# The third mixer's input products in three rounded passes, its weights through the ring of pieces, and the recurrence's rates moved ahead of the queries

## The reference

```python
def even_mixer_2(h, pos, w_in, conv_w, conv_b, w_a, b_a, w_i, b_i, lam, q_norm, k_norm, sinks, w_out):
    proj = h @ w_in                       # h is the normed input, w_in is 1024 x 1792
    xb, gate, q, k, v = jnp.split(proj, cuts, axis=-1)      # 512, 512, 512, 128, 128 columns
    y_lru = rg_lru(xb, conv_w, conv_b, w_a, b_a, w_i, b_i, lam) * jax.nn.gelu(gate)
    q = rope(rms_norm_2(q.reshape(bsz, seq, 8, 64), q_norm), pos)
    k = rope(rms_norm_2(k.reshape(bsz, seq, 2, 64), k_norm), pos)
    y_att = sliding_window_attention(q, k, v, sinks)
    return jnp.concatenate([y_lru, y_att], axis=-1) @ w_out

def rg_lru(xb, ...):
    xc = causal_depthwise_conv_2(xb, conv_w) + conv_b
    r = sigmoid(xc by 8 blocks @ w_a + b_a);  gi = sigmoid(xc by 8 blocks @ w_i + b_i)
    log_a = -8.0 * r * softplus(-lam)
    a = exp(log_a);  u = sqrt(-expm1(2 log_a)) * (gi * xc)
    h_t = a_t * h_(t-1) + u_t             # a scan over the tokens
```

## Time and profile before

| | us |
|---|---|
| median of 3 runs | 2619.16 (2617.56 to 2625.74) |
| the profiled execution | 2622.34 |
| its span | 2620.5 |
| PE busy in the span | 2438.7 (93%) |
| DVE, ACT, POOL busy | 1805.9, 1424.2, 321.3 |
| stage mix2, first input product to the start of its attention | 1079.2 to 1134.3 |

### The profile page before, as it was taken

The page is one execution under the profiler, slowest core; times in us unless marked ns, Lnnn a source line. Parts: engine busy times, 40 slices in busy tenths (PEclk is TensorE's granted clock), DMA queues, the critical chain, the costliest instruction groups (busy, mean ns, idle before and its releaser), DMA issues. The chain is left out here.

```text
span 2620.5 us, 40002 instructions
## 1 busy us (share of the span) xinstructions
PE 2438.7 (93%) x15188; PEld 2039.8 (78%) x15188; DVE 1805.9 (69%) x2444; ACT 1424.2 (54%) x1900; POOL 321.3 (12%) x215
## 2 busy tenths in 40 slices
PE   7889889989897999989998996899999999999998
PEld 6447569989885799757997985788888888888886
DVE  3665554557575555574556764889989988889986
ACT  4242243445552444343435542677778787877776
POOL 4110200014442000000003431000000000000000
PEclk9889999999899999979998997899999999999999
DMA  7510325544231454414544402899999999999995
GB/s 256 174 47 21 128 97 191 176 142 152 97 129 65 138 177 166 165 65 145 192 160 168 155 2 93 322 373 383 378 384 367 389 376 381 377 379 377 377 381 214
DMA packets 180011, 573.86 MB, mean 219 GB/s; under 512 B 11966, under 2 KB 81726, under 8 KB 136764
## 3 DMA queue, kind: packets, MB, share of 16 engines
q1 hardware_dynamic: 175932, 558.27, 57.4%
q0 software_dynamic: 2992, 11.01, 1.6%
q10 hardware_dynamic: 976, 3.03, 0.3%
HBM read 564.16 MB, written 6.29 MB: 218 GB/s over the span
## 5 line engine op out<-in xcount | busy, mean ns | idle before, releaser
L3487 DVE TENSOR_TENSOR moe_weights_low<-ring,moe_weights_high 128x1024 fp32r<-128x1024 f32 x672 | 780.4, 1221 | 95.3 <-ACT moe_weights_high L3736 95.2
L3736 ACT CAST moe_weights_high<-ring 128x1024 fp32r<-128x1024 f32 x672 | 686.7, 1053 | 109.1 <-PE banks L258 106.1
L256 PE MATMUL banks<-moe_weights_high,moe_rows_high 128*128 128x512 f32 x896 | 355.7, 397 | 3.1 <-DVE moe_rows_low L3492 2.5
L258 PE MATMUL banks<-moe_weights_low,moe_rows_high 128*128 128x512 f32 x896 | 350.9, 392 | 0.0
L257 PE MATMUL banks<-moe_weights_high,moe_rows_low 128*128 128x512 f32 x896 | 350.2, 391 | 0.0
L256 PE MATMUL banks<-ffn_x_high,ffn_weights_high 128*128 128x256 f32 x1056 | 299.5, 284 | 0.7 <-DVE ffn_x_low L3110 0.7
L257 PE MATMUL banks<-ffn_x_high,ring_low 128*128 128x256 f32 x1056 | 298.0, 282 | 0.0
L258 PE MATMUL banks<-ffn_x_low,ffn_weights_high 128*128 128x256 f32 x1056 | 297.7, 282 | 0.0
L3286 DVE TENSOR_TENSOR ring_low<-ring,ffn_weights_high 128x2048 fp32r<-128x2048 f32 x60 | 134.8, 2289 | 127.7 <-ACT ffn_weights_high L3260 127.7
L256 PEld LDWEIGHTS banks<-ffn_x_high,ffn_weights_high 128*128 128x128 f32 x1056 | 199.6, 189 | 4.2 <-DVE ffn_x_low L3110 1.3
L257 PEld LDWEIGHTS banks<-ffn_x_high,ring_low 128*128 128x128 f32 x1056 | 199.9, 189 | 2.7
(11 more groups left out here) (626 smaller groups left out, 4632.1 us busy)
## 6 DMA issues: line engine op xcount, KB each, us to landing
ring<-in_moe_gate_pieces SPq DMA_DIRECT2D x112, 1024.0 KB, 7.1
ring<-in_moe_up_pieces SPq DMA_DIRECT2D x112, 1024.0 KB, 7.4
ring<-in_moe_down_pieces SPq DMA_DIRECT2D x112, 1024.0 KB, 7.2
ring<-in_ffn_w SPq DMA_DIRECT2D x66, 1024.0 KB, 7.7
ring<-in_od_w_in SPq DMA_DIRECT2D x10, 2048.0 KB, 8.2
ring<-in_o_w_in SPq DMA_DIRECT2D x8, 2048.0 KB, 8.5
ring<-in_e_ffn_w_gate SPq DMA_DIRECT2D x11, 1024.0 KB, 5.4
ring<-in_e_ffn_w_up SPq DMA_DIRECT2D x11, 1024.0 KB, 7.9
```

Source lines behind the costliest of these rows:

```text
L256: pe.matmul(out_, lh, rh, start=start, stop=False)
L258: return pe.matmul(out_, lh, rl, start=False, stop=stop)
L3487: dve.tensor_tensor(lo[:, b], piece, hi[:, b].bitcast(F32), ALU.subtract).then_inc(sems["lo_done"], 1)
L3736: act.copy(hi[:, b * 1024:(b + 1) * 1024], piece).then_inc(sems["hi_done"], 1)
```

## The change

The product `project_parts` is cut in two: `begin_parts` makes the pieces and can split the first of them early, and `project_parts` can take what has been begun. All four input products of the stage become three-pass products on `x_parts`. Two of the first product's pieces are split inside the norm. After the first piece of keys and values the four pieces of the queries are split (`during={0: ...}`); after the third piece of the queries the four pieces of the gate product (`during={2: gate_early}`). `decay_rates` and `one_less` are emitted ahead of the queries' product, and `square_root` becomes the first entry of the attention's `during` list. In `project_parts` both token tiles of a product end together, with the last piece.

```diff
-        def project_parts(lhs, n_k, w, n_cols, ready, take, first_col=0, after=None, during={}):
+        def begin_parts(n_k, w, n_cols, first_col, after=None):
             rows = P
             chunk = 512 if n_k <= 8 else 256
...
+            def first_pieces(count):
+                for i in range(count):
+                    split_one(i)
+                for i in range(count):
+                    parts_ready[i] = split[i][2]()
+            return pieces, split, parts_ready, slot_of_chunk, split_one, first_pieces
+
+        def project_parts(lhs, n_k, w, n_cols, ready, take, first_col=0, after=None, during={}, begun=None):
+            rows = P
+            begun = begin_parts(n_k, w, n_cols, first_col, after) if begun is None else begun
+            pieces, split, parts_ready, slot_of_chunk, split_one, first_pieces = begun
+
             def first_piece():
-                split_one(0)
-                parts_ready[0] = split[0][2]()
+                first_pieces(1)
...
-        def turned_parts(w, first_col, n_tiles):
+        def turned_parts(w, first_col, n_tiles, ahead=2):
...
             def early():
-                for i in range(2):
+                for i in range(ahead):
                     split_one(i)
-                for i in range(2):
+                for i in range(ahead):
                     parts_ready[i] = split[i][2]()
...
-            normed = norm_turned(h, D, None, xT, g_in, params_landed, lambda: None)
+            w_in = a["e_w_in_2"][0]
+            first_early, first_product = turned_parts(w_in, 0, NT4)
+            normed = norm_turned(h, D, None, x_parts, g_in, params_landed, first_early)
+            top[0] = keep
...
-            conv_project(a["e_w_in_2"][0], 0, NT4, taps, bias, params_landed, normed, ACT.Identity, finish)
+            conv_project(w_in, 0, NT4, taps, bias, params_landed, normed, ACT.Identity, finish, first_product)
...
-            project(xT, KD, a["e_w_in_2"][0], 2 * KVH * N, normed, copy_out(qkv[:, :, H * N:]), first_col=2 * LW + H * N)
+            query_parts = begin_parts(KD, w_in, H * N, 2 * LW)
+            project_parts(x_parts, KD, w_in, 2 * KVH * N, normed, copy_out(qkv[:, :, H * N:]), first_col=2 * LW + H * N,
+                          during={0: lambda: query_parts[-1](4)})
...
             def take_queries(ps, mark, t, c0, n):
                 if t == 0:
-                    decay_rates()
-
                     @block.scalar
...
-                sums = query_sums(0, made["queries"])
-                one_less()
-                query_scaled(0, sums)
+                query_scaled(0, query_sums(0, made["queries"]))
...
-            project(xT, KD, a["e_w_in_2"][0], H * N, normed, take_queries, first_col=2 * LW)
-            sums = query_sums(1, V.at())
-            square_root()
-            rotated = query_scaled(1, sums)
+            decay_rates()
+            one_less()
+            gate_early, gate_product = turned_parts(w_in, LW, NT4, 4)
+            project_parts(x_parts, KD, w_in, H * N, normed, take_queries, first_col=2 * LW, during={2: gate_early},
+                          begun=query_parts)
+            rotated = query_scaled(1, query_sums(1, V.at()))
...
-            project_turned(a["e_w_in_2"][0], LW, NT4, normed, take)
+            gate_product(w_in, LW, NT4, normed, take)
...
-                                    const("band"), sinks, [lambda: None, inputs, gated_scan])
+                                    const("band"), sinks, [square_root, inputs, gated_scan])
```

More of the change, by code:

```diff
@@ L4054, in take @@
                 return S.at()
-            project_turned(a["e_w_in_2"][0], LW, NT4, normed, take)
+            assert top[0] <= ARENA - KD * T - PIECES * PIECE, top[0]
+            gate_product(w_in, LW, NT4, normed, take)
             gate_ready = S.at()
             have = paired_attention(qkv, H, KVH, N, N ** -0.5, lambda i: y[:, :, i * N:(i + 1) * N], rotated,
-                                    const("band"), sinks, [lambda: None, inputs, gated_scan])
+                                    const("band"), sinks, [square_root, inputs, gated_scan])
             lru_ready = made["lru"]
```

## The result

The changed kernel takes 2631.44 us (median of 6 runs, 2628.0 to 2636.08) against 2621.33 for the kernel before in the same comparison: a ratio of 1.004, 95% interval 1.0025 to 1.0055. It is slower, by 10.1 us at the medians. The interval (6.6 to 14.4 us) is clear of zero; its lower end lies under the 0.3%, 7.9 us, that the prediction counts as no change, and its middle over it. One of the six runs before took 5200.5 us and stands outside the ratio; the other five have a median of 2619.16, and the 15 to 20 runs of the kernel before in each later comparison have medians of 2620.48 to 2623.44. The profiled execution has a span of 2630.0, 9.5 more than before.

A forecast was written before the change was run, and what follows sets the result against it. VectorE's queue was taken to set the stage's end; +6.4 us to decay_rates, +2.6 to the rotation and +0.65 in the attention made +9.7, so 2628.9 us from the median 2619.2, range 2619 to 2637.

The forecast's parts named there:

- L968 at 1143: Sign for being right: VectorE's last rotation in the stage at 1143 us; before 1138 would show the prediction wrong.
- What bounds: In mix2, VectorE's queue, fed by ScalarE and TensorE, sets the stage's end, though TensorE looks full.
- The norm: Start of the stage: a subtraction and eight L445 make x^T ready at 1081.5 us, +2.3.
- The first product: After the norm: product takes 11.4 us, VectorE's convolutions set x_ready, which does not move; nothing gained.
- The keys' wait: Keys and values: casts queue behind the convolution's last copy, TensorE idles 5.5 us, product ends +3.9 us.
- half clock: Keys' product after TensorE's idleness: five us at clock 0.50 add 2.5 us, bounds 0 and 5.7.
- Rates to rotation: From decay_rates to rotated: 29.3 us instead of 26.7, +2.6, including 4.3 for two gate subtractions.
- The attention: square_root's 5.3 us mostly fill VectorE's 4.74 us idle before its first scores; +0.65 us, bounds 0 and 2.
- The lock: VectorE and GpSimd on shared SBUF ports: slowing each other is shown, a full lock for the whole instruction is not.
- The whole pace arrives: Rival: TensorE's queue sets the stage's end, so its savings arrive; about -6 us, 2613; chance 7%.
- Covered: Rival: subtractions at 1.23 and 2.41 alone, no clock drop; +5 to +6 us, 2625, no measurable change; chance 35%.

The follow-up runs named there:

- e1: Changed kernel with the two pieces of keys and values split inside the first product; stage 103.7 us, ratio 1.0044 to the kernel before.
- e8: Kernel before with all but one reciprocal of square_root's VectorE work moved into the attention's first round; 2615.97 us, ratio 0.9977, stage 91.5 us.
- e2: Changed kernel with all 14 subtractions of the stage on VectorE, none on GpSimd; stage 103.4 us, ratio 1.0037 to the kernel before.
- e3: Changed kernel with the first GpSimd subtraction waiting for VectorE's scaling and first subtraction; stage 104.1 us, ratio 1.0025 to the kernel before.
- e4: Changed kernel with the gate product's subtractions between sums and scaling of the queries' tile 0; stage 107.0 us, ratio 1.0044 to the kernel before.
- e10: Kernel before with two unused GpSimd subtractions on SBUF added, beside convolutions and beside the scaling of the queries' tile 0; stage 96.2 us, one run.
- e7: Changed kernel with e1, e3, e4 and one square_root reciprocal between tile 1's sums and scaling; stage 103.0 us, ratio 1.0021 to the kernel before.

## Why the prediction was right

It forecast +9.7 us, slower, with VectorE's queue as the cause; measured were +10.1 at the medians and +11.4 in the stage. The waits stood where it had put them, with the releasers that it named, but for one step, the first product; two steps came near by sizes that were not as stated, and that part is luck. So is the match of the absolute times that it gave as signs (L968 at 1143, measured 1142.47): the stage began 2.8 us earlier and was that much longer. Step by step:

*What bounds.* Right. e1 gave TensorE 6.3 us and the stage took 2.7 of them; e8 touched only VectorE's order, and the way from `decay_rates` to `rotated` shortened by 3.4 of the 3.5 us moved off it.

*The norm, +2.3.* Measured +3.0, and by another mechanism. I let the subtraction stand at 2.88 between the scaling and L445. It took 1.21; the scaling itself was held by GpSimd's, 3.76 for 1.67. e2 and e3 put it back to 1.68. That the sum came near was luck: one term was 1.7 too long, another, 2.1, was missing.

*The first product, +0 at `x_ready`.* This step failed: +2.1. The prediction let VectorE's convolutions set `x_ready`, with the product done in 11.4 us at full clock. The last three convolutions each waited 0.73 us for TensorE, which began 3.0 us later and took 13.1 us for the 14.1 of before (1079.44 to 1092.55), its first 3.6 us mostly at half clock. So the product made up for 1.0 us where 2.6 were forecast. e3, with x^T 2.0 earlier, has `x_ready` at 22.9, but its product too begins at half clock. All eight profiles with the three passes in this stage have 2.8 us or more at 0.50 in the first product, and of the four with plain products only e8's has, which speaks for the change as the cause of most of this loss; e8's 25.0, without any edit there, says that it can also come by the state of the clock alone. What about the change brings it is not separated here.

*The keys' wait, +3.9, with half clock +2.5.* Right in place and releaser, and the gap was 4.83 for 5.5. The keys' subtraction was alone, 1.23. Their product took 7.2 us for 5.7 (1097.38 to 1104.6), so the half clock cost 1.5. `decay_rates` came +8.2 for +6.4; the 1.8 between them is nearly the 2.1 by which `x_ready` was late. The queries' two subtractions were 3.0 each as said; L760 took 1.09 for 0.29 beside GpSimd.

*Rates to rotation, +2.6.* Measured +2.8. The gate's two subtractions took 4.66 for 4.3, the powers left 1.75 idle each.

*The attention, +0.65.* Measured +0.45.

*The lock.* I weighed the Trainium skill's "SBUF — State Buffer", section "SBUF: two separate sides", against the earlier trace rows and wrote that a full lock is not shown. e4 and e10 show VectorE held until GpSimd is done, and to take as evidence against that was wrong. The 3.6 us for a pair that I worked out from the Trainium skill's rule is an estimate, and the pairs of the earlier trace rows at 3.0 and 3.1 are shorter; why is not shown. Yet the rule is what made e4 and e7 miss. What I had to ask was not what a pair of subtractions costs but which other VectorE instructions will meet GpSimd's. The same section of the Trainium skill says that a VectorE operation in a two-port mode takes the lock too. That would fit the scaling, which reads one tile and took 3.76, if it ran in such a mode; no run here shows the mode.

*The rivals.* "The whole pace arrives" is out by e1. "Covered" would have had pieces at 1.23 and no drop of the clock; e2, with its subtractions at 1.2 us each and none beside GpSimd, still costs 8.4 us in the stage.

## What to carry to other kernels

A busier engine is not the bound of a stage if another one's queue ends later: speed up TensorE only after following what VectorE and ScalarE must do first, and count each cast and subtraction that feeds it on their queues, at the place where it is emitted. Before giving GpSimd a share of VectorE's work, look at what VectorE does beside it: here the convolution's, which read PSUM and one SBUF tile, went on, and those on two SBUF tiles stood still. And look for one short instruction to put into each wait (a reciprocal over a power on GpSimd): in e8 that gained 0.23%, where a new form of four products lost 0.4%.

## What the runs showed of the hardware

A GpSimd subtraction of 128 x 1024 holds a VectorE multiplication on two SBUF tiles until it is done (0.69 us became 2.72, 2.78 and 2.88, beside GpSimd instructions of 2.6 to 2.7) and a convolution step on PSUM not at all (0.55 and 1.52, unchanged). A scaling of one SBUF tile, four instructions of 128 x 512, went from 1.68 to 3.76 us beside one. Six subtractions on VectorE alone took 6.9 us, two beside GpSimd's 6.0. With the same instructions ahead of it, TensorE's first product in this stage took 14.0 us at the full clock and 15.9 where the granted clock was 0.50 to 0.59 in its first 4 us (e8).
